# A RWKV time-mixing kernel: two head groups carried side by side through the chunk inverse, and a group norm that no longer takes its mean

## The chip, the cores and the metric

One core of one Trainium2 chip runs the whole program. Times are device microseconds (us) of one execution. Engines are named as in the profile: PE (TensorE matmuls), PEld (its weight loads), DVE (VectorE), ACT (ScalarE), POOL (GpSimd), SP (SyncE, which issues the weight transfers). PSUM is the memory PE writes; it has eight banks of 512 fp32 words a partition.

## What is computed

A block of 256 tokens with 1024 channels goes through a first block and then four layers; layers 0 and 3 mix over time with RWKV-7 (16 heads of 64 channels), and only this part is changed. In the reference, for each head and token:

```
def step(state, inp):
    r_t, w_t, k_t, v_t, kk_t, a_t = inp
    sa = jnp.einsum('bhvk,bhk->bhv', state, -kk_t)
    state = (state * w_t[:, :, None, :]
             + sa[..., None] * (kk_t * a_t)[:, :, None, :]
             + v_t[..., None] * k_t[:, :, None, :])
    return state, jnp.einsum('bhvk,bhk->bhv', state, r_t)
...
mean = jnp.mean(y, axis=-1, keepdims=True)
var = jnp.mean(jnp.square(y - mean), axis=-1, keepdims=True)
y = ((y - mean) * lax.rsqrt(var + RW_GN_EPS)).reshape(bsz, seq, d) * ln_w + ln_b
bonus = jnp.sum(rh * kh * r_k, axis=-1, keepdims=True) * vh
out = ((y + bonus.reshape(bsz, seq, d)) * g).astype(h.dtype) @ w_o
```

The mean and the variance are over a head's 64 values of one token. `y` is linear in `v`, channel by channel of the head.

## The kernel before

The program is a chain of stages. Each is a block of its own: every engine runs its list of instructions in order, waits on counted semaphores, and all meet at the block's end. A layer with time mixing runs a feed-forward half, `rwkv_wide_stage` (r, v, k), `rwkv_scale_stage` (decays and scalings, L2633 to L2828), `rwkv_chunk_stage` (L2831), `rwkv_norm_stage` (L3242), `output_stage` and the other feed-forward half.

**The chunk stage** cuts the 256 tokens into two chunks of 128 and the 16 heads into two groups of 8, so four pairs n = (chunk, group) are worked through one after the other. For a pair it needs the inverse of a unit-triangular 128x128 matrix per head. That is built from the two 64x64 diagonal blocks: PE makes the products of a and b (L2882, and transposed L2892), DVE masks them out of PSUM (L3138, L3139) and makes the first level of the inverse T and of its transpose (L3146 to L3154, `first_level`). Then come five levels, each doubling the size of the inverted blocks:

- POOL masks the matrix for the level (L3124), PE multiplies it with T (`level_x`, 16 products of 64x64, L3003), ACT copies the result to SBUF (L3074);
- PE multiplies back for T (L3013; not in the fifth level) and for its transpose (L3018), 16 products of 64x64 each, and DVE adds these (L3182, L3184, `level_sums`). The next `level_x` waits for both sums.

A level is thus one chain PE, ACT, PE, DVE. The rest of a pair's work (turning k, b and v to token-major, L2904; the products with k, L2917, and their masked copies, L3161; the products for c, L2941, for u, L2954, with b and r, L2923, for the carry, L2961, for y, L2977 and L2978, and for the state) is put between the level steps of the *next* pair, by hand, in the loop over n at the end of the PE, ACT and DVE lists. So the first pair's inverse has nothing beside it, and the last pair's other products come alone after the last level. PSUM: the levels use banks 0 to 2, the rest banks 3 to 7.

**The norm stage** sums each head's y per token on PE (L746 in `sums_by_token`, 16 products of 128x128 by 128x2), scales (DVE L3289), spreads the mean back (PE L755 in `spread_by_token`), subtracts it (DVE L3292), squares (ACT L3282), sums the squares (PE L746 again), takes the inverse root (DVE L3294, ACT L3284, DVE L3296), spreads it (L755), multiplies, adds the bonus and gates (DVE L3308, L3301, L3303).

**Weights** come through a ring of four slots of 3 MB, `load_ahead` (L439) on SP's queue; a unit waits until the one four before it is freed. The scale stage issues up to the unit three past its own last one (L2652). Units 62 and 63 (layer 0) hold the output weights; 64, the third past, is the next feed-forward half's first. The scratch of the chunk stage is one idle ring slot and three of the ten 1 MB buffers.

Of the kernel before, what the change touches and what calls it, by code (L numbers as in the profile page):

```python
# [22 lines left out]
P = 128  # L23
SEQ = 256
# [2588 lines left out]
def rwkv_scale_stage(core, n, h, dx, x_w, x_g, x_a, r, k, v, lw, a, g):  # L2613
# [19 lines left out]
    with core.nc.Block() as block:  # L2633
# [197 lines left out]
def rwkv_chunk_stage(core, r, k, v, a, b, level_bufs, solve_buf, wide):  # L2831
# [5 lines left out]
    ab_, t_, tt, ab21 = ([piece(level_bufs, 4 * n + q) for n in range(2)] for q in range(4))  # L2837
    x_, masked, c_in, u_ = (piece(solve_buf, q) for q in range(4))
    ak_t, rk_t, rb_t = (wide[:, q * 1024:(q + 1) * 1024].rearrange("p (h t) -> p h t", h=8) for q in range(3))
    tok = wide[:, 3072:4608].rearrange("p (q c m) -> p q c m", q=3, c=4)  # L2840
    state = core.state[:, 0, :].rearrange("p (c m) -> p c m", m=HEAD)
    scaled = core.state[:, 1, :].rearrange("p (c m) -> p c m", m=HEAD)
    bank = lambda q: core.psum[:, q, :]
    zeros = core.zeros
# [4 lines left out]
    groups = [(ck, g) for ck in range(SEQ // P) for g in range(2)]  # L2849
    N, L = len(groups), LEVELS - 1  # L2850
# [5 lines left out]
    pairs_of = lambda banks: banks.rearrange("p b (c t) -> p c b t", c=4)  # L2856
    turned_half = lambda h, half: other[half.start] if h % 2 else half
    with core.nc.Block() as block:
        names = ("turned", "turned_sb", "ab_products", "ab_sb", "ba_products", "t_ready", "k_products", "k_sb",
                 "rb_products", "rb_sb", "level_mask", "level_x", "level_x_sb", "level_t", "level_t_sb", "level_tt",  # L2860
                 "level_tt_sb", "c_sums", "c_sb", "u1_sums", "u1_sb", "carry_sums", "carry_sb", "u2_sums", "u2_sb",
# [4 lines left out]

        @block.tensor
        def _(pe):
            def rows(x, n, h):
                ck, g = groups[n]  # L2870
                return x[HEAD * (h % 2):HEAD * (h % 2) + HEAD, 4 * g + h // 2, ck * P:(ck + 1) * P]

            def a_and_r(n, h):
                ck, g = groups[n]
                at = (4 * g + h // 2) * SEQ + ck * P
                return core.bufs[HEAD * (h % 2):HEAD * (h % 2) + HEAD, 0:5:4, at:at + P]

            def products_ab(n):
                if n >= 2:
                    wait(pe, "rb_sb", n - 1)  # L2880
# [15 lines left out]
            def turn_operands(n):  # L2896
                ck, g = groups[n]
                now = slice(ck * P, (ck + 1) * P)
                if n:
                    wait(pe, "y_sb", n)  # L2900
# [912 lines left out]
```

## Time and profile before

| what | value |
|---|---|
| three runs | 3466.52, 3467.67, 3473.76 us; median 3467.67 |
| profiled execution, first to last instruction (span) | 3464.7 us; its own device time is not listed, so the median's 3.0 us more is taken as what lies around a span |
| busy, share of the span | PE 91%, PEld 85%, DVE 67%, ACT 46%, POOL 4% |
| chunk stage, layers 0 and 3 | 154.2 and 144.7 us |
| norm stage, layers 0 and 3 | 25.2 and 25.3 us |

A PE row's x counts two passes for an fp32 product (L3003's 16 products are x32) and one for a transpose. Its busy time is start to modelled end; groups overlap a little at their ends, so a group's cost in PE's queue is read from its start to the next group's start. PEclk is the granted clock of PE: 1.00 is 2.4 GHz, 0.50 is 1.2 GHz.

### The profile page before, as it was taken

The page shows a single profiled execution, that of the slowest core. Times are in us where ns is not written, and L with a number is a line of the kernel's source. Part 1 is how long each engine was busy: PE and PEld are TensorE (multiplying, and loading weights), DVE is VectorE, ACT ScalarE, POOL GpSimd, SP SyncE. Part 2 cuts the span into 40 slices and gives each one's busy share as a digit, 9 for nine tenths or more (in the row PEclk, how much of TensorE's full clock was granted, in tenths as well). Part 3 has the DMA queues.
Part 4 walks back from the last instruction along what each step waited for, and adds up shares of the span by engine and source line. Part 5 has one row for each costly group of instructions (what it writes and reads, how often), then busy time and mean ns, then how long its engine had stood idle before and what let it go on. Part 6 is the DMA issues. An engine that isn't in the chain of part 4 may idle for free. (4 is left out here: it accounts for less than half of the span.)

```text
span 3464.7 us, 62893 instructions
## 1 busy us (share of the span) xinstructions
PE 3157.3 (91%) x26416; PEld 2942.4 (85%) x26416; DVE 2335.4 (67%) x3486; ACT 1580.8 (46%) x2255; POOL 130.5 (4%) x148
## 2 busy tenths in 40 slices
PE   7679999889987799999989899999899999978899
PEld 5568777789876789999987899999699998867899
DVE  6547999767774467677577577775667677564544
ACT  3326777644551244544552444444644444432443
POOL 0000000000102000000000000000000001011000
PEclk9778999989997989999996899999899999989899
DMA  9336999757520047677430277675157575310242
GB/s 391 138 134 263 368 370 365 291 211 303 204 104 2 2 191 305 244 289 295 173 146 1 116 281 277 249 303 194 40 226 303 224 304 227 112 38 2 110 183 85
DMA packets 74502, 698.32 MB, mean 202 GB/s; under 512 B 8096, under 2 KB 12192, under 8 KB 50848
## 3 DMA queue, kind: packets, MB, share of 16 engines
q1 hardware_dynamic: 31360, 533.52, 39.3%
q10 hardware_dynamic: 41760, 153.11, 11.6%
q0 software_dynamic: 1152, 8.39, 0.6%
q8 instruction: 173, 2.83, 0.3%
q14 instruction: 57, 0.47, 0.0%
HBM read 690.79 MB, written 4.19 MB: 201 GB/s over the span
## 5 line engine op out<-in xcount | busy, mean ns | idle before, releaser
L1186 DVE TENSOR_TENSOR w_split<-ring,w_split 128x1024 fp32r<-128x1024 f32 x513 | 626.3, 1223 | 407.6 <-ACT w_split L1097 405.1
L1097 ACT ACTIVATE w_split<-ring 128x1024 fp32r<-128x1024 f32 x513 | 540.6, 1056 | 774.7 <-PE banks L1027 580.6
L1025 PE MATMUL banks<-u_split,w_split 128*128 128x256 f32 x2816 | 805.7, 286 | 14.7 <-DVE u_split L1246 12.9
L1026 PE MATMUL banks<-u_split,w_split 128*128 128x256 f32 x2816 | 803.8, 285 | 0.0
L1027 PE MATMUL banks<-u_split,w_split 128*128 128x256 f32 x2816 | 803.5, 285 | 0.0
L1025 PEld LDWEIGHTS banks<-u_split,w_split 128*128 128x128 f32 x2816 | 548.2, 195 | 19.4 <-DVE w_split L1186 10.0
L1026 PEld LDWEIGHTS banks<-u_split,w_split 128*128 128x128 f32 x2816 | 548.1, 195 | 0.4
L1027 PEld LDWEIGHTS banks<-u_split,w_split 128*128 128x128 f32 x2816 | 547.7, 195 | 0.0
L584 DVE CUSTOM_DVE_ANT_0 bufs<-bufs 128x1024 f32<-128x1024 f32 x332 | 395.0, 1226 | 41.9 <-DMA bufs<-ada 25.0
L1025 PE MATMUL banks<-h_split,w_split 128*128 128x256 f32 x1408 | 398.7, 283 | 1.8 <-DVE w_split L1186 1.8
L1026 PE MATMUL banks<-h_split,w_split 128*128 128x256 f32 x1408 | 398.4, 283 | 0.0
L1027 PE MATMUL banks<-h_split,w_split 128*128 128x256 f32 x1408 | 398.4, 283 | 0.0
L520 PE MATMUL banks<-bufs_split,ring_split 128*128 128x256 f32 x1312 | 381.0, 290 | 0.0
L518 PE MATMUL banks<-bufs_split 128*128 128x256 f32 x984 | 293.4, 298 | 55.2 <-DVE ring_split L506 37.1
L2129 DVE TENSOR_TENSOR ring_split<-ring,bufs_split 128x1024 fp32r<-128x1024 f32 x240 | 293.9, 1266 | 22.8 <-ACT bufs_split L2010 22.3
L519 PE MATMUL banks<-bufs_split 128*128 128x256 f32 x936 | 275.2, 294 | 0.0
L1025 PEld LDWEIGHTS banks<-h_split,w_split 128*128 128x128 f32 x1408 | 270.3, 192 | 2.5 <-issue 2.5
L1026 PEld LDWEIGHTS banks<-h_split,w_split 128*128 128x128 f32 x1408 | 270.3, 192 | 0.0
L1027 PEld LDWEIGHTS banks<-h_split,w_split 128*128 128x128 f32 x1408 | 270.3, 192 | 0.0
L2010 ACT ACTIVATE bufs_split<-ring 128x1024 fp32r<-128x1024 f32 x240 | 250.1, 1063 | 32.7 <-PE banks L1876 29.3
L520 PEld LDWEIGHTS banks<-bufs_split,ring_split 128*128 128x128 f32 x1312 | 262.5, 200 | 0.0
L518 PEld LDWEIGHTS banks<-bufs_split 128*128 128x128 f32 x984 | 199.9, 203 | 65.4 <-DVE ring_split L506 40.1
(472 smaller groups left out, 5067.5 us busy)
## 6 DMA issues: line engine op xcount, KB each, us to landing
ring<-stream SPq DMA_DIRECT2D x155, 3072.0 KB, 10.9
bufs<-ada ACTq DMA_DIRECT2D x288, 512.0 KB, 10.6
bufs<-ada SPq DMA_DIRECT2D x7, 2048.0 KB, 11.9
bufs<-ada POOLq DMA_DIRECT2D x8, 1024.0 KB, 8.3
ring<-stream SPq DMA_DIRECT2D x2, 2688.0 KB, 9.7
bufs<-c_rows SPq DMA_DIRECT2D x9, 512.0 KB, 4.5
ring<-stream SPq DMA_DIRECT2D x1, 2704.0 KB, 12.9
ring<-stream SPq DMA_DIRECT2D x1, 2176.0 KB, 7.8
```

Source lines behind the costliest of these rows:

```text
L518: pe.matmul(out, w_high, x_high, start=start, stop=False, skip_group_check=True)
L519: pe.matmul(out, w_high, x_low, start=False, stop=False, skip_group_check=True)
L520: return pe.matmul(out, w_low, x_high, start=False, stop=stop, skip_group_check=True)
L584: dve.tensor_tensor_reduce(w, w, c_row, 1.0, 0.0, ALU.mult, ALU.add, into).then_inc(done.sem, 1)
L1025: pe.matmul(out, w(0), x(0), start=start, stop=False, skip_group_check=True)
L1026: pe.matmul(out, w(0), x(1), start=False, stop=False, skip_group_check=True)
L1027: return pe.matmul(out, w(1), x(0), start=False, stop=stop, skip_group_check=True)
L1097: nc.scalar.activation(w_split[:, slot, 0, :], piece(j, b), ACT.Copy).then_inc(high.sem, 1)
L1186: e = nc.vector.tensor_tensor(w_split[:, slot, 1, :], piece(j, b), w_split[:, slot, 0, :].bitcast(F32), ALU.subtract)
L2010: act.activation(w_high[number % 4], piece(j, b), ACT.Copy).then_inc(high.sem, high.count(1))
L2129: dve.tensor_tensor(low_piece(j, b), piece(j, b), w_high[number % 4].bitcast(F32), ALU.subtract)\
```

## The change

- The two groups of a chunk go through the inverse side by side: each level does `level_x` for group 0 and 1, other products of both groups, the products back for group 0 and 1, other products again. Group g has PSUM banks 2g and 2g+1 for the levels and 4+2g and 5+2g for the rest; every scratch tile exists once a group.
- The first chunk's inverse now has its own turning and its products with k, with b and r, and the next chunk's ab and ba beside it; the second chunk's has the first's c, u, carry, y and state products, then its own turning and products with k. The second chunk's c, u, rb, carry and y products for both groups come after the last level.
- The ab and ba products are made as 64x64 blocks, only those that are used (24 and 16 a group in place of 8 and 8 of 128x128); DVE takes them with one full-width instruction in place of two half-width ones.
- v is turned by a matmul with `centering`, the identity less each head's mean, in place of a transpose, so y comes out with mean zero. One DVE instruction makes `centering`. ACT writes y's square beside y (one more activation a pair).
- The norm stage loses the mean: its sum, scale, spread, subtraction and squares. Its ACT list adds the first bias, takes the root, then adds the other biases.
- The scratch takes a second ring slot, so unit last + 3 is issued in the norm stage and no longer in the scale stage.

```diff
-            core.load_ahead(sync, (f"g2{n}", 1))
+            core.load_ahead(sync, None, core.place[(f"g2{n}", 1)][0] + SLOTS - 1)
...
-                    last = pe.matmul(bank(6 + h % 2)[:, (h // 2) * P:(h // 2 + 1) * P], rows(b, n, h), rows(a, n, h),
+                    for half in blocks:
+                        pe.matmul(banks(g)[half, h % 2, pair_at(h)], rows(b, n, g, h, half), rows(a, n, g, h, half), start=True, stop=True)
+                    last = pe.matmul(banks(g)[lower, h % 2, second_at(h)], rows(b, n, g, h, lower), rows(a, n, g, h, upper),
                                      start=True, stop=True)
...
+            def turn_v(n, g):
+                wait(pe, "padded", 1)
+                wait(pe, "kb_turned_sb", through(n, g))
+                for c in range(4):
+                    last = pe.matmul(banks(g)[:, 0, c * P:(c + 1) * P], v[:, 4 * g + c, n * P:(n + 1) * P], centering,
...
+            def level_x(n, g, level):
+                wait(pe, "level_mask", level_through(n, g, level))
                 if level == 1:
-                    wait(pe, "t_ready", n + 1)
-                else:
-                    wait(pe, "level_t_sb", n * (L - 1) + level - 1)
-                if m:
-                    wait(pe, "level_tt_sb", m)
+                    wait(pe, "t_ready", through(n, g))
+                if n or level > 1:
+                    wait(pe, "level_t_sb", level_through(n, g, level) - 2)
                 for h in range(8):
                     for half in blocks:
-                        last = pe.matmul(bank(1 + h % 2)[turned_half(h, half), pair_at(h)], masked[half, h, :], t_[n % 2][half, h, :],
+                        last = pe.matmul(level_banks(g)[turned_half(h, half), h % 2, pair_at(h)], masked[g][half, h, :], t_[g][half, h, :],
                                          start=True, stop=True)
                 done(last, "level_x")
 
-            def level_t(n, level):
-                m = n * L + level - 1
-                wait(pe, "level_x_sb", m + 1)
+            def level_t(n, g, level):
+                wait(pe, "level_x_sb", level_through(n, g, level))
                 if level < L:
                     for h in range(8):
                         for half in blocks:
-                            last = pe.matmul(bank(h % 2)[turned_half(h, half), pair_at(h)], tt[n % 2][half, h, :], x_[half, h, :],
+                            last = pe.matmul(level_banks(g)[turned_half(h, half), h % 2, pair_at(h)], tt[n][g][half, h, :], x_[g][half, h, :],
                                              start=True, stop=True)
-                    done(last, "level_t")
-                for h in range(8):
-                    for half in blocks:
...
+            behind_x = ({1: turn_k_and_b, 2: lambda n, g: products_with_k(n, g, 0), 3: products_rb,
+                         4: lambda n, g: products_ab(n + 1, g), 5: lambda n, g: products_ba(n + 1, g)},
+                        {1: lambda n, g: c_products(n - 1, g), 2: lambda n, g: carry_products(n - 1, g), 3: lambda n, g: y_products(n - 1, g),
+                         4: turn_k_and_b, 5: lambda n, g: products_with_k(n, g, 0)})
+            behind_t = ({1: turn_v, 2: lambda n, g: products_with_k(n, g, 1)},
+                        {1: lambda n, g: u_products(n - 1, g, 0), 2: lambda n, g: u_products(n - 1, g, 1),
+                         3: lambda n, g: state_products(n - 1, g), 4: turn_v, 5: lambda n, g: products_with_k(n, g, 1)})
+            for n in range(2):
+                for level in range(1, LEVELS):
+                    for g in both:
+                        level_x(n, g, level)
+                    for g in both:
+                        behind_x[n][level](n, g)
+                    for g in both:
+                        level_t(n, g, level)
+                    if level in behind_t[n]:
+                        for g in both:
+                            behind_t[n][level](n, g)
+            for g in both:
+                c_products(1, g)
+            for g in both:
+                u_products(1, g, 0)
+            for g in both:
+                products_rb(1, g)
+            for g in both:
+                carry_products(1, g)
+            for g in both:
+                u_products(1, g, 1)
+            for g in both:
+                y_products(1, g)
...
+                    act.activation(here(squares), y, ACT.Square)
+                    done(act.activation(here(r), y, ACT.Copy), "y_sb")
...
+            for g in both:
+                ab_copies(0, g)
+                first_level(0, g)
+            done(dve.scalar_tensor_tensor(centering, core.const("heads"), -1.0 / HEAD, ident, ALU.mult, ALU.add), "padded")
+            level_sums(0, 1)
+            k_copies(0, 0)
+            level_sums(0, 2)
+            k_copies(0, 1)
+            rb_copies(0)
+            level_sums(0, 3)
+            for g in both:
+                ab_copies(1, g)
+            level_sums(0, 4)
+            level_sums(0, 5)
+            for g in both:
+                first_level(1, g)
+            level_sums(1, 1)
+            carries(0)
+            level_sums(1, 2)
+            level_sums(1, 3)
+            states()
+            level_sums(1, 4)
+            k_copies(1, 0)
+            level_sums(1, 5)
+            k_copies(1, 1)
+            rb_copies(1)
+            carries(1)
     core.end_stage()
...
-                last = sums_by_token(core, pe, y, c, 0, RW_HEADS)
-            last.then_inc(mean.sem, mean.count(1))
-            pe.wait_ge(mean_ready.sem, mean_ready.at(1))
-            for c in range(KC):
-                last = spread_by_token(core, pe, mean_bank(c // 2)[:, c % 2, :], values, c, RW_HEADS)
-                if c % 2:
-                    last.then_inc(mean_spread.sem, mean_spread.count(1))
-            for c in range(KC):
-                pe.wait_ge(squared.sem, squared.at(c // 2 + 1))
-                last = sums_by_token(core, pe, tmp, c, 5, RW_HEADS)
+                last = sums_by_token(core, pe, squares, c, 5, RW_HEADS)
             last.then_inc(summed.sem, summed.count(1))
...
-            for q in range(KC // 2):
-                act.wait_ge(centered.sem, centered.at(q + 1))
-                act.activation(pair(tmp, q), pair(cent, q), ACT.Square).then_inc(squared.sem, squared.count(1))
...
+            with_bias(0)
             act.wait_ge(scaled.sem, scaled.at(1))
             act.activation(values, values, ACT.Sqrt).then_inc(rooted.sem, rooted.count(1))
+            for q in range(1, KC // 2):
+                with_bias(q)
...
-            dve.wait_ge(mean.sem, mean.at(1))
-            dve.tensor_scalar(values, core.psum[:, 0, 0:2 * RW_HEADS], -1.0 / HEAD, None, ALU.mult).then_inc(mean_ready.sem, mean_ready.count(1))
-            for q in range(KC // 2):
-                dve.wait_ge(mean_spread.sem, mean_spread.at(q + 1))
-                dve.tensor_tensor(pair(cent, q), pair(y, q), mean_bank(q), ALU.add).then_inc(centered.sem, centered.count(1))
...
-                dve.scalar_tensor_tensor(cent[:, c, :], cent[:, c, :], core.col(f"ln_w{n}")[:, c:c + 1], root_bank(c), ALU.mult, ALU.mult)\
+                dve.scalar_tensor_tensor(cent[:, c, :], y[:, c, :], core.col(f"ln_w{n}")[:, c:c + 1], root_bank(c), ALU.mult, ALU.mult)\
```

How the instructions stand on PE, in order. The names: `bufs` and `ring` are SBUF scratch, `banks` is PSUM. First place, the first two levels of the first inverse, from the ba products on. Before:

```order
L2892 MATMUL banks<-bufs 128x128 x8
L3003 MATMUL banks<-bufs 64x64 x16
L3013 MATMUL banks<-bufs 64x64 x16
L3018 MATMUL banks<-bufs 64x64 x16
L3003 MATMUL banks<-bufs 64x64 x16
L3013 MATMUL banks<-bufs 64x64 x16
L3018 MATMUL banks<-bufs 64x64 x16
```

Now:

```order
L3016 MATMUL banks<-ring 64x64 x32
L2915 MATMUL banks<-consts_sb,bufs 128x128 x16
L3025 MATMUL banks<-ring 64x64 x16
L3033 MATMUL banks<-ring 64x64 x16
L3025 MATMUL banks<-ring 64x64 x16
L3033 MATMUL banks<-ring 64x64 x16
L2922 MATMUL banks<-small,bufs 128x128 x8
L3016 MATMUL banks<-ring 64x64 x32
L2933 MATMUL banks<-bufs 128x256 x8
L3025 MATMUL banks<-ring 64x64 x16
L3033 MATMUL banks<-ring 64x64 x16
L3025 MATMUL banks<-ring 64x64 x16
```

L3016, L3025 and L3033 are the old L3003, L3013 and L3018, for two groups; L2915 turns k and b, L2922 turns v, L2933 is the old L2917. They stood behind the second pair's levels.

Second place, what PE does after the last level, up to the products for y. Before, one group (the other was done beside the last inverse):

```order
L2904 MATMUL banks<-consts_sb,bufs 128x128 x12
L2917 MATMUL banks<-bufs 128x256 x8
L2936 MATMUL banks<-zeros_split 128x256 x2
L2938 MATMUL banks<-state,bufs 128x64 x8
L2941 MATMUL banks<-ring 128x64 x8
L2954 MATMUL banks<-bufs 64x64 x8
L2923 MATMUL banks<-bufs 128x128 x8
L2961 MATMUL banks<-bufs 64x64 x8
L2954 MATMUL banks<-bufs 64x64 x8
L2972 MATMUL banks<-zeros_split 128x512
L2974 MATMUL banks<-bufs,state 64x128 x8
```

Now, both groups, behind the last L3033 and L2933:

```order
L2955 MATMUL banks<-zeros_split 128x256 x2
L2957 MATMUL banks<-state,bufs 128x64 x8
L2960 MATMUL banks<-ring 128x64 x8
L2955 MATMUL banks<-zeros_split 128x256 x2
L2957 MATMUL banks<-state,bufs 128x64 x8
L2960 MATMUL banks<-ring 128x64 x8
L2973 MATMUL banks<-ring 64x64 x16
L2942 MATMUL banks<-bufs 128x128 x16
L2981 MATMUL banks<-bufs,spare 64x64 x16
L2973 MATMUL banks<-ring 64x64 x16
L2991 MATMUL banks<-zeros_split 128x512
L2993 MATMUL banks<-bufs,state 64x128 x8
```

L2955, L2957, L2960 make c, L2973 u, L2942 the products with b and r, L2981 the carry, L2991 and L2993 begin y. Turning and the products with k no longer stand here, but everything from c on stands here for two groups.

Third place, SP's queue in layer 0, as one piece of the difference; L2633 ends the scale stage, L3269 and L3262 begin and end SP's list of the norm stage:

```order
 L2650 UNCONDITIONAL_BRANCH
 L452 DMA ring<-stream 128x2048
+L2633 UNCONDITIONAL_BRANCH
+L3269 UNCONDITIONAL_BRANCH
 L452 DMA ring<-stream 128x6144
-L2633 UNCONDITIONAL_BRANCH
+L3262 UNCONDITIONAL_BRANCH
 L1723 UNCONDITIONAL_BRANCH
 L452 DMA ring<-stream 128x6144 x2
```

The 3 MB transfer moves past the scale and the chunk stage into the norm stage.

## Rows read from the trace of the kernel before

**Rows 1.** Stretches: chunk and norm stages; last two, chunk stages up to the clock's rise.

```profile
core 0: us, PE busy (x) PEld busy (x) DVE busy (x) ACT busy (x) POOL busy (x), PEclk, DMA share, GB/s
1035.20:1189.40 154.20, 119.88 (x2614) 106.55 (x2614) 69.97 (x120) 29.91 (x56) 25.39 (x20) 0.82 0.03 10
1189.40:1214.60 25.20, 18.13 (x192) 17.57 (x192) 11.97 (x23) 7.33 (x14) 0.00 (x0) 0.79 0.01 2
3058.70:3203.40 144.70, 109.98 (x2614) 97.02 (x2615) 69.94 (x120) 29.93 (x57) 25.39 (x20) 0.90 0.01 2
3203.40:3228.70 25.30, 18.13 (x192) 17.55 (x192) 11.98 (x23) 7.31 (x14) 0.00 (x0) 0.85 0.00 1
1035.20:1066.50 31.30, 20.91 (x428) 19.33 (x430) 11.50 (x18) 2.39 (x4) 6.33 (x5) 0.50 0.10 41
3058.70:3078.30 19.60, 11.70 (x224) 10.71 (x224) 8.75 (x14) 1.19 (x2) 3.80 (x3) 0.51 0.01 2
```

**Rows 2.** Timeline, layer 3, a level at the low clock (start us, us, engine, ...).

```profile
3067.18 1.13 PE L3003 MATMUL banks<-bufs 64*64 64x64 f32 x32 [4.69 <-DVE bufs L3154]
...
3069.02 1.13 PE L3013 MATMUL banks<-bufs 64*64 64x64 f32 x32 [0.71 <-ACT bufs L3074]
...
3069.93 1.92 PE L3018 MATMUL banks<-bufs 64*64 64x64 f32 x32
...
3072.73 1.13 PE L3003 MATMUL banks<-bufs 64*64 64x64 f32 x32 [0.88 <-DVE bufs L3184]
```

**Rows 3.** Timeline, layer 3, a level with other products beside it, full clock.

```profile
3112.36 0.69 PE L3003 MATMUL banks<-bufs 64*64 64x64 f32 x32
...
3113.18 0.60 ACT L3074 ACTIVATE bufs<-banks 128x512 f32<-128x512 f32 x1 [2.76 <-PE banks L3003]
...
3113.83 0.69 PE L3013 MATMUL banks<-bufs 64*64 64x64 f32 x32 [0.32 <-ACT bufs L3074]
...
3114.35 1.10 PE L3018 MATMUL banks<-bufs 64*64 64x64 f32 x32
...
3115.49 0.69 DVE L3184 TENSOR_TENSOR bufs<-bufs,banks 128x512 f32<-128x512 f32 x1 [0.21 <-PE banks L3018]
```

**Rows 4.** Timeline, layer 3, from the ba products' copies to the next inverse's start.

```profile
3090.15 1.39 DVE L3146 TENSOR_TENSOR bufs<-banks,consts_sb 64x512 f32<-64x512 f32 x2 [0.40 <-PE banks L2892]
...
3094.27 0.69 PE L3003 MATMUL banks<-bufs 64*64 64x64 f32 x32 [4.17 <-issue]
...
3094.90 2.80 PE L2904 MATMUL banks<-consts_sb,bufs 128*128 128x128 f32 x12
```

**Rows 5.** Timeline, layer 3, the last pair's products, one after the other.

```profile
3178.07 0.51 PE L2972 MATMUL banks<-zeros_split 128*128 128x512 f32 x1
...
3181.58 0.60 ACT L3074 ACTIVATE bufs<-banks 128x512 f32<-128x512 f32 x1 [4.03 <-PE banks L2978]
...
3182.23 1.53 PE L2904 MATMUL banks<-consts_sb,bufs 128*128 128x128 f32 x12 [0.69 <-ACT bufs L3074]
...
3183.69 2.38 PE L2917 MATMUL banks<-bufs 64*128 64x256 f32 x16
...
3184.87 2.53 DVE L3161 TENSOR_TENSOR ring<-banks,consts_sb 128x512 f32<-128x512 f32 x4 [5.34 <-PE banks L2917]
...
3187.46 0.50 PE L2936 MATMUL banks<-zeros_split 128*128 128x256 f32 x2 [1.39 <-DVE ring L3161]
...
3188.93 2.00 PE L2941 MATMUL banks<-ring 128*128 128x64 f32 x16
...
3192.18 0.68 PE L2954 MATMUL banks<-bufs 64*64 64x64 f32 x16 [1.25 <-ACT bufs L3085]
...
3192.79 1.16 PE L2923 MATMUL banks<-bufs 64*128 64x128 f32 x16
```

**Rows 6.** Timeline, layer 0, norm stage: first and second sum, the root.

```profile
1189.43 3.70 PE L746 MATMUL banks<-consts_sb,bufs 128*128 128x2 f32 x32 [0.94 <-PEq L2858]
...
1198.73 3.73 PE L746 MATMUL banks<-consts_sb,bufs 128*128 128x2 f32 x32
...
1200.22 1.28 ACT L3284 ACT_TABLE_LOAD   x1
1202.50 0.19 DVE L3294 TENSOR_SCALAR small<-banks 128x32 f32<-128x32 f32 x1 [2.96 <-PE banks L746]
```

**Rows 7.** Page, DMA issues: size and us from issue to landing.

```profile
ring<-stream SPq DMA_DIRECT2D x155, 3072.0 KB, 10.9
```

More of the change, by code:

```diff
@@ L2828, in rwkv_scale_stage, with rwkv_chunk_stage @@
     core.end_stage()
-def rwkv_chunk_stage(core, r, k, v, a, b, level_bufs, solve_buf, wide):
+def rwkv_chunk_stage(core, r, k, v, a, b, squares, wides, tails, rest, centering):
     s = core.small
@@ L2896, in turn_operands, with products_ba @@
[L2896 to L2900, printed above, removed]
-                wait(pe, "t_ready", min(n + 2, N))
-                for q, (x, to) in enumerate(((k, 3), (b, 4), (v, 5))):
-                    for c in range(4):
-                        last = pe.transpose(bank(to)[:, c * P:(c + 1) * P], x[:, 4 * g + c, now], ident)
+            def products_ba(n, g):
+                out = banks(g) if n else level_banks(g)
+                if n:
+                    wait(pe, "ab_sb", through(n, g))
+                for h in range(8):
+                    for half in blocks:
+                        last = pe.matmul(out[half, h % 2, pair_at(h)], rows(a, n, g, h, half), rows(b, n, g, h, half), start=True, stop=True)
+                done(last, "ba_products")
@@ new lines, in turn_k_and_b @@
+            def turn_k_and_b(n, g):
+                if n:
+                    wait(pe, "y_sb", through(n - 1, g))
+                    wait(pe, "state_sb", through(n - 1, g))
+                else:
+                    wait(pe, "ab_sb", through(n, g))
+                for q, x in enumerate((k, b)):
+                    for c in range(4):
+                        last = pe.transpose(banks(g)[:, q, c * P:(c + 1) * P], x[:, 4 * g + c, n * P:(n + 1) * P], ident)
+                done(last, "kb_turned")
@@ L2915, in products_with_k, with products_rb @@
                 for h in range(4 * part, 4 * part + 4):
                     at = (h // 2 - 2 * part) * SEQ
-                    last = pe.matmul(bank(first + h % 2)[:, at:at + SEQ], rows(k, n, h), a_and_r(n, h), start=True, stop=True)
+                    last = pe.matmul(banks(g)[:, h % 2, at:at + SEQ], rows(k, n, g, h), a_and_r(n, g, h), start=True, stop=True)
                 done(last, "k_products")
-            def products_rb(n):
-                wait(pe, "c_sb", n + 1)
+            def products_rb(n, g):
+                if n:
+                    wait(pe, "u1_sb", through(n, g))
+                else:
+                    wait(pe, "k_sb", 4 * n + 2 + g + 1)
@@ L3141, in first_level @@
[L3141 to L3147 removed]
+            spread = lambda m: m.unsqueeze(1).unsqueeze(1).to_broadcast([m.shape[0], 4, 2, HALF])
@@ L3186, in scale_state @@
-            def scale_state(n):
-                ck, g = groups[n]
-                if ck:
+                for g in both:
+                    wait(dve, "k_products", 4 * n + 2 * part + g + 1)
+                    heads = slice(4 * part, 4 * part + 4)
+                    sums = banks(g).rearrange("p b (c a t) -> p c b a t", c=2, a=2)
+                    for out, which in ((ak_t[g], 0), (rk_t[g], 1)):
+                        last = dve.tensor_tensor(by_pair(out[:, heads, :]), sums[:, :, :, which, :],
+                                                 causal[:, which, :].unsqueeze(1).unsqueeze(1).to_broadcast([P, 2, 2, P]), ALU.mult)
+                    done(last, "k_sb")
```

461 lines of the change are left out of this document (200 added, 261 removed).

## The prediction, made before the change was run

> **What bounds the kernel now.** I read the stretches first, stage by stage. The two chunk stages take 154.2 and 144.7 us and the two norm stages 25.2 and 25.3 [rows 1]; the rest of the program is not touched. In a chunk stage DVE is busy 70 of 145 us, ACT 30, POOL 25 and PE 110, so no engine is full; DMA is near zero, so weights don't bound it. PE's clock is the second thing to see: 0.50 in the first 31.3 us of layer 0's stage and the first 19.6 us of layer 3's [rows 1], where the first inverse runs alone; 0.82 and 0.90 over the stages. The timeline then shows what a level costs. Alone and at the low clock, from one L3003 to the next, it is 5.55 us, of which PE's queue works 0.91 (L3013) and some 1.9 (L3018) and about 1.1 (L3003), the rest being ACT's copy, DVE's sum and the handovers [rows 2]. At the full clock, with others' products between, the same steps are 0.52 (L3003, L3013) and 1.03 (L3018), and the chain from L3003 to L3013 is 1.47, 0.60 of it ACT [rows 3]. So the stage is a chain of latencies, four pairs one after another, with a bare inverse at the front and a bare pair of product groups at the back (3182.23 to 3203.4, 21 us). The norm stage is a plain chain too.
>
> **The norm stage.** Between the first sum's start and the second's lie 9.30 us [rows 6], and nothing else than the mean is in them: sum, scale, spread, subtraction, squares. They go; the second sum and all behind it stay. ACT could be late with the root: its table load now comes after two biases (0.8), so it ends at 2.1 us after the start, and the scale is due 3.77 after its sum's start (L746 to L3294) [rows 6]. Covered. The other six biases run beside PE's spread. Term: 2 x -9.3 = -18.6. If the load ended late, its 1.28 would show, once a stage.
>
> **Costs of product groups at full clock,** start to next start, for one group of heads: turning 12 tiles 1.46, so 0.12 each; k products 2.3 for both parts; c in the first chunk 1.9, in the second 3.4 (from L2936 on: 1.47 + 1.9); u 0.6; rb 1.1; y in the second chunk 3.25 (from L2972 to ACT's copy, less the handover), in the first, where the state is zero, some 1.8; k's masked copies on DVE 2.55 [rows 5]. Carry: as u, 0.6. Four inverse products back (two groups) T = 2 x (0.52 + 1.03) = 3.1; two `level_x` X = 1.0 [rows 3].
> New forms, bounded: a 64x64 product costs 0.032 where the sixteen spread over all four quarters of the array (L3013) and 0.065 where they use two (L3018) [rows 3]. The 24 of ab use three quarters in turn: between 0.8 and 1.6 a group, I take 1.2, near the old 1.1. The 16 of ba use all four: 0.5 to 1.0, I take 0.55. State, 16 products on two quarters, 1.0. v by matmul: between a transpose's 0.12 and twice L2941's 0.24 [rows 5], I take 0.24, so 1.0 a group, where transposes were 0.5. DVE's full-width copies: 0.69 as L3184's 128x512, not 1.39 as L3146's two [rows 3, 4]; so a first level is 4.0 - 0.7 = 3.3 and ab copies 1.4. `centering` 0.35 on DVE, covered; the square, 0.60 of ACT, is covered but for one at the end.
>
> **The new chunk stage, marked at each start of the products back.** Head, low clock: ab 2.4 (1.2 at half rate); DVE in line for both groups 1.4 + 3.3 + 1.4 + 3.3, with handovers 9.6; second `level_x` 0.9; 16 turnings at 2.80/12 = 0.23 [rows 4], 3.6. Together 16.5. Then
> - first chunk, level 1 to 2: T 3.1, v 1.9, X 1.0, k 2.3 = 8.3; to 3: 3.1 + k 2.3 + X 1.0 + rb 2.2 = 8.6;
> - to 4, with nothing behind T: the second group waits T 3.1, handovers 0.4, two sums 1.4, its own X 0.5, = 5.4; ab 2.4: 7.8; to 5: 5.4 + ba 1.1 = 6.5;
> - to the second chunk: PE waits for DVE, first products 1.3 with handover, sums 1.4 + 0.3, two first levels 6.6, X 0.6, c 3.8 = 14.0;
> - to 2: T 3.1, u 1.2, X 1.0, carry 1.2 = 6.5; to 3: 3.1 + u 1.2 + X 1.0 + y 3.6 = 8.9; to 4: 3.1 + state 2.0 + 1.0 + turning 2.0 = 8.1; to 5: 3.1 + v 1.9 + 1.0 + k 2.3 = 8.3;
> - behind: L3033 2.1, k 2.3, wait for copies 0.5, c 6.8, ACT's copies and u 2.1, rb, its copy and the carry 4.5, the carry's copy and u 1.8, y 6.5, square and copy 1.5 = 28.1.
> Sum 16.5 + 105.1 = 121.6. Two checks: the same bookkeeping with the old order and layer 3's clock gives 145 against 144.7 measured; and PE's queue alone, summed, is about 97, so 122 is not impossible.
> Beside it the clock. Both old stages fell low again after PE stood idle: after the 4.17 us of one first level the next 2.80 us of turning ran at about half rate [rows 4]. The new stage has one such hole, twice as long, before the second chunk, and small ones at the end. A stretch of 7 us at half rate there costs 1.5 to 2.5. And the first rise came at 19.6 in one layer and 31.3 in the other; PE is dense in the new stage from 12 us on, so I take about 16 in one and 20 to 25 in the other, 2 to 3 more. Layer 3: 123; layer 0: 126. Bounds: 118 (full clock from the start) and 133 (low to 32 us, and twice again).
> Terms: 123 - 144.7 = -21.7, 126 - 154.2 = -28.2.
>
> **The rest.** Where the stall goes: the last level's end is now followed by 28 us in one line, where 26 were before, so the tail doesn't shrink; it is the third and fourth pair's chains that vanish. The weight unit issued in the norm stage lands 10.9 us after issue [rows 7], inside the 16 us left of it, and it is the next feed-forward half's; the output stage, which comes between, has its units. So 0. If that cover failed it would be up to 10.9 a layer. ACT, DVE and POOL work beside PE.
>
> **Sum.** -18.6 - 21.7 - 28.2 = -68.5 on the profiled span of 3464.7: 3396. The median of the runs is 3.0 above that span, so 3399 us.
>
> **Rivals.**
> - DVE becomes the bound. For: both groups' sums (2.8) and both groups' masked k copies (5.1, in two halves) are in one in-order list, so a copy of other work stands ahead of a sum that `level_x` waits for; by my marks the copies of level 2 end 0.1 us before the sum is due. Against: DVE totals 65 of 122 (70 less the copies and first levels that shrink, four times 1.4). The Trainium skill (TensorEngine Tiling (Array Packing), PSUM Bottleneck) says that packing speeds up TensorE but not the evacuation of PSUM, which may then bound; the 4.17 us hole agrees with it. Price: half a k copy (1.3) at each of ten levels, 13 a stage, 3425.
> - PE's quarters get in each other's way (ab 1.6, ba 1.0, v 0.45 each): over four pairs 1.6 + 1.8 + 3.4, about 7 a stage, 3413. Inside the range.
> - Side by side only in name: the groups' waits serialise them. Then only the norm's term is left: 3449. Against: own banks, tiles and counts for each group.
> - The slower side: PE idles in each wait often enough that its clock stays at 0.50 through the stage. All PE costs are then about 1.8 times (L3018 1.9 for 1.03), and by the same marks a stage takes 190: 380 - 299 - 18.6 = +62, 3530. It decides from 159 us a stage on, some 107 us of it low. For: 31 us low in layer 0. Against: PE has more work in less time, and the old stage of layer 3 had 0.90 with less. The Trainium skill (TensorE: Matmul & The Clock Gate, Part 1) reports a kernel whose short idles between product groups made the clock swing between its two levels; the drop in [rows 4] agrees in kind.
> - The clock rises at once and stays: 118 a stage, 3386.
>
> **Chances.** Forecast, within 3388 to 3416, 0.81; above, up to 3449, 0.11; below 3388, 0.06; slower 0.02. Range 3388 to 3416: it takes in both clock bounds but the ends, and the quarters' case. A change of under 0.2% (7 us) can't be told from none here; so faster 0.97, same 0.01, slower 0.02.
>
> **What would show it.** After: chunk stages of 120 to 128 us; L3016's x32 runs close together, with the pairs of ACT copies; PE idle some 7 us before the second chunk's second `level_x`, broken only by the first, and DVE busy there; PEclk near 0.95 after the first 20 us; the norm stage at 16 us; no wait on the ring's first unit behind the output stage. Wrong: DVE copies ahead of late sums (L3192 in place of the sums) at most levels, or PEclk at 0.50 past 40 us.

## Result, and the profile after

| | before | after |
|---|---|---|
| median (range, runs) | 3467.1 (3461.9 to 3473.8, 4) | 3411.9 (3408.0 to 3413.3, 4) |
| profiled span | 3464.7 | 3406.2 |
| ratio of times | | 0.985, 95% interval 0.9833 to 0.9866 |

The forecast was 3399, in 3388 to 3416. The kernel is 55 us faster where 68 were forecast. First the windows of the changed kernel (us of the stretch, then busy time and count of PE, PEld, DVE, ACT and POOL, PE's clock, DMA share, GB/s): chunk and norm stage of layer 0, of layer 3, and two stretches inside layer 3's chunk stage.

```profile
1034.56:1163.33 128.77, 106.12 (x2822) 98.17 (x2823) 66.62 (x113) 31.40 (x61) 25.26 (x20) 0.87 0.01 3
1163.33:1180.90 17.57, 10.45 (x97) 10.15 (x97) 9.20 (x19) 4.79 (x10) 0.00 (x0) 0.77 0.46 180
3020.69:3153.07 132.38, 109.14 (x2822) 100.98 (x2823) 66.72 (x113) 31.41 (x61) 25.33 (x20) 0.85 0.01 3
3153.07:3170.16 17.09, 10.20 (x96) 9.88 (x97) 9.03 (x18) 4.79 (x11) 0.00 (x0) 0.78 0.47 185
3077.50:3094.60 17.10, 13.94 (x218) 13.58 (x220) 5.42 (x8) 3.47 (x8) 2.53 (x2) 0.50 0.01 2
3094.60:3142.20 47.60, 43.59 (x1171) 40.19 (x1166) 25.11 (x49) 15.45 (x30) 7.52 (x6) 1.00 0.01 3
```

The chunk stages took 128.8 and 132.4 us (154.2 and 144.7 in [rows 1]), the norm stages 17.6 and 17.1 (25.2 and 25.3). That is 25.4 + 12.3 + 7.6 + 8.2 = 53.5 of the 58.5 us between the spans. The other 5.0 lie in code that is the same: in the twelve profiles of the changed kernel and its variants the first chunk stage starts between 1031.2 and 1041.4 us, so a time of the whole program moves by that much on its own, and the experiments below are read by their stages. A stage moves too: the unedited changed kernel's four chunk stages in two profiles (e8_after_again is the second) took 128.8, 132.4, 130.8 and 129.0 us. A gain of some 3 us in the mean of two stages is thus only just above that spread.

The fifth row is the surprise: 17.1 us in the middle of the stage at a clock of 0.50, with PE busy 13.9 of them. It will be called the low stretch, and the place ahead of it, between the two chunks, where PE waits twice, the hole. Here is the hole in layer 3's timeline (start, us, engine, line, ...): DVE's first levels for the second chunk (L3167 to L3175), `level_x` of either group (L3016) and the first chunk's c products (L2960).

```profile
3073.67 0.69 DVE L3207 TENSOR_TENSOR ring<-ring,banks 128x512 f32<-128x512 f32 x1 [0.24 <-PE banks L3033]
3074.27 0.68 DVE L3167 TENSOR_TENSOR ring<-banks,consts_sb 128x512 f32<-128x512 f32 x1
...
3075.30 0.85 DVE L3171 TENSOR_TENSOR ring<-ring,consts_sb 64x256 f32<-64x256 f32 x2
...
3076.80 0.69 DVE L3175 TENSOR_TENSOR ring<-ring,consts_sb 128x512 f32<-128x512 f32 x1
3077.40 0.69 DVE L3167 TENSOR_TENSOR ring<-banks,consts_sb 128x512 f32<-128x512 f32 x1
...
3077.59 1.13 PE L3016 MATMUL banks<-ring 64*64 64x64 f32 x32 [3.96 <-DVE ring L3175]
...
3078.43 1.93 DVE L3171 TENSOR_TENSOR ring<-ring,consts_sb 64x256 f32<-64x256 f32 x2
3078.82 1.26 POOL L3145 TENSOR_TENSOR ring<-ring,consts_sb 128x512 f32<-128x512 f32 x1 [6.53 <-PE banks L3016]
...
3081.01 0.68 DVE L3175 TENSOR_TENSOR ring<-ring,consts_sb 128x512 f32<-128x512 f32 x1
...
3081.80 1.13 PE L3016 MATMUL banks<-ring 64*64 64x64 f32 x32 [3.07 <-issue]
...
3082.86 7.09 PE L2960 MATMUL banks<-ring 128*128 128x64 f32 x32
```

PE waits 3.96 us for DVE, does one `level_x` and waits 3.07 more. Then the 16 c products (x32, two passes each) take 7.09 us; at the full clock the same take 3.8 (below). And L3171's two instructions are 0.85 for group 0 and 1.93 for group 1, where POOL's mask (L3145) runs beside them from 3078.82 on.

The stage against the forecast, step by step (from one start of the products back to the next, us; the first from the stage's first product):

| step | forecast | layer 0 | layer 3 |
|---|---|---|---|
| head | 16.5 | 17.9 | 17.9 |
| level 1 to 2 / 2 to 3 | 8.3 / 8.6 | 8.3 / 7.9 | 8.5 / 7.9 |
| 3 to 4 / 4 to 5 | 7.8 / 6.5 | 6.7 / 7.1 | 9.2 / 7.3 |
| to the second chunk (the hole) | 14.0 | 20.0 | 18.3 |
| 1 to 2 | 6.5 | 8.2 | 7.9 |
| 2 to 3 / 3 to 4 / 4 to 5 | 8.9 / 8.1 / 8.3 | 9.2 / 8.0 / 7.9 | 10.8 / 8.0 / 7.9 |
| behind the last level (the tail) | 28.1 | 27.4 | 28.6 |
| sum | 121.6 | 128.8 | 132.4 |

Where others' products stand beside the levels the forecast holds within 1.1 us, but for two steps of layer 3: 9.2 for 7.8 and 10.8 for 8.9. In these PE stands still in the middle of its products for 2.04 us, and for 1.10 and 0.57 us, with nothing it waits for (last section). The excess is 1.4 at the head and 6 to 8 in the hole and the step behind it; in layer 0 a standstill of 1.51 us just ahead of the hole is in it.

### The profile page after: what moved, and what is told of

The parts are those of the page before. It is cut to its first block and busy times, and to the rows that moved or that the text cites. A ratio compares the mean times of both kernels' runs of the same rounds, so it can differ in the third digit from the quotient of the medians.

```text
span 3406.2 us, 63313 instructions
## 1 busy us (share of the span) xinstructions
PE 3120.0 (92%) x26640; PEld 2917.2 (86%) x26640; DVE 2322.7 (68%) x3462; ACT 1578.9 (46%) x2255; POOL 130.3 (4%) x148
## 6 DMA issues: line engine op xcount, KB each, us to landing
ring<-stream SPq DMA_DIRECT2D x1, 2704.0 KB, 13.7
```

## The experiments

Each is an edit of the changed kernel. Three theories of the excess: A, PE's clock behind the hole; B, DVE's copies in their one list; C, the time that the products themselves take in PE's queue. D is a part of the hole: POOL's mask beside DVE.

### Filling the hole, and its sizes

```diff
+            def fill(count):
+                wait(pe, "level_t_sb", level_through(0, 1, L))
+                for q in range(count):
+                    pe.matmul(level_banks(1)[:, q % 2, second_half], ident, v[:, q % 4, :], start=True, stop=True)
...
+                        if n and level == 1:
+                            fill((5, 6)[g])
                         level_x(n, g, level)
```

> Adds 11 products of 128x128 by 128x256 that nobody reads on PE before the second chunk: 5 before its first level_x of group 0 (after the last sum), 6 before that of group 1, into level banks that nobody reads then. Nothing waits longer for them unless they outlast DVE (11 x 0.43 at the full clock, 4.7 us of 7.0 idle). Theory A (the 12.4 us between my schedule and layer 3's measured stage is mostly a clock that stays at 0.50 for 17 us after PE's hole): the low stretch of 17 us behind the hole shrinks or goes, the row of the c products (7.09 us) falls to about 4, and a stage is 4 to 8 us shorter, the program 3396 to 3404. Theory B (DVE's copies and handovers are the excess): the clock may rise, the time stays within 2 us of 3412. Theory C (the excess is in PE's queue): 2 x 1 us slower, 3413 to 3416.

Measured: median 3408.4 (3393.6 to 3414.7), ratio 0.982 (0.9788 to 0.9852). The windows are its two chunk stages, the norm stage of layer 0, the hole's stretch and 13.6 us of layer 3's tail:

```profile
1039.63:1169.88 130.25, 112.81 (x2845) 102.72 (x2845) 66.72 (x113) 31.54 (x61) 25.35 (x20) 0.88 0.01 3
3031.98:3160.00 128.02, 112.59 (x2844) 102.98 (x2845) 66.63 (x113) 31.53 (x61) 25.34 (x20) 0.87 0.01 3
1169.88:1185.65 15.77, 8.76 (x96) 8.43 (x96) 9.02 (x18) 4.79 (x10) 0.00 (x0) 0.84 0.51 201
3081.90:3095.00 13.10, 10.85 (x154) 9.41 (x154) 7.90 (x13) 2.79 (x7) 2.54 (x2) 1.00 0.01 3
3133.20:3146.80 13.60, 13.40 (x112) 12.41 (x113) 1.54 (x2) 3.46 (x8) 0.00 (x0) 0.50 0.00 0
```

and rows of layer 3's timeline: added products, the c products of the first chunk, and of the tail's second group:

```profile
3086.50 2.86 PE L3023 MATMUL banks<-bufs,consts_sb 128*128 128x256 f32 x12
...
3090.71 3.79 PE L2960 MATMUL banks<-ring 128*128 128x64 f32 x32
...
3136.68 3.67 PE L2960 MATMUL banks<-ring 128*128 128x64 f32 x16
```

The clock stayed at 1.00 through the hole. The hole's step and the one behind it took 16.3 + 5.8 us in layer 0 and 14.6 + 5.8 in layer 3, against 28.2 and 26.2: **6 us less a stage**, and with the full clock layer 3's two steps are 20.4, as forecast (20.5). So A is right on what the low stretch costs. It is wrong on the stage, and on the time of 3396 to 3404: the clock fell in the tail instead, where only 0.53 us of idle stood ahead, the second group's L2960 took 3.67 (2.0 at full clock), and the tail 34.1 us for 27.4. What was won in the middle was given back. C finds nothing here: 4.7 us of added products lengthened neither step.

> e1_fill_hole with 60 and 80 products of 64x64 by 64x64 (0.032 us each, 4.5 us) in place of 5 and 6 of 128x128 by 128x256. There the clock stayed full at the hole and fell 45 us later, in the c products of the tail, for 13.7 us, with nothing but 0.5 us of idle ahead. If the size of the added products had brought that on: here no fall at 101 to 104 us of the stage, tail of 23 us, stages of 122 to 124 us. If it is the long stretch at the full clock: the same fall, stages of 128 to 130. If small products don't count as work for the clock: the 14 to 17 us low behind the hole stay.

Edit: the same `fill`, with products of 64x64 in turn over the four quarters, `fill((60, 80)[g])`. Median 3403.3 (3395.9 to 3410.1). Layer 3 did as before: full through the hole (14.9 + 5.8), then 13.6 us at 0.50 from 100.4 us of the stage on, tail 34.2, stage 127.3. The fall in the tail is thus not due to large products. Small ones did as well as large ones in layer 3, where 3.4 us of idle remained in three pieces; in layer 0, where 3.7 remained in four, the clock fell for 10.2 us behind the hole: stage 131.5.

> The changed kernel unedited, for its times beside the others on one chip and for a second profile. Theory A: 17 us at 0.50 behind the hole in both layers again, the full clock in the tail's c products, stages of 128 to 132 us. Rival: the clock's pattern is chance, and the low stretch is absent or elsewhere in one of the two layers.

Median 3417.1 (3409.9 to 3420.2, 6 runs); stages 130.8 and 129.0; 17.1 and 13.6 us low behind the hole, the tail's c products at the full clock. So A's pattern is no chance of one profile; the length of the low stretch varies, 13.6 or 17.1.

### The first level made earlier

```diff
+            for g in both:
+                first_tt(1, g)
+            for g in both:
+                first_t(1, g)
             level_sums(0, 5)
-            for g in both:
-                first_level(1, g)
```

(`first_tt` is the part of `first_level` that needs ab alone, `first_t` the part on the ba products.)

> The second chunk's first level is made on DVE before the last sums of the first chunk and no longer behind them: its transposed part after the sums of level 4, the rest as the ba products come. PE's hole (3.96 + 3.07 us of layer 3's stage) falls to about 1.5 us. Theory A: the hole's 5.5 us and the 6 to 8 us of low clock behind it both go, 10 to 13 us a stage, 3386 to 3392. Theory B (DVE is the bound): the same instructions only stand elsewhere in the list, the wait turns up before level 5's sums: 0 to 3 us a stage, 3406 to 3412. Without a clock effect: 5.5 us a stage, 3401.

Measured: median 3410.9 (3403.6 to 3416.9), stages 125.8 and 128.2. The hole fell from 7.0 to 3.9 and 4.8 us, and 13.7 us of low clock stayed behind it in both layers. Layer 3's timeline says why no more:

```profile
3075.21 0.96 DVE L3175 TENSOR_TENSOR ring<-ring,consts_sb 128x256 f32<-128x256 f32 x1
...
3076.18 1.83 DVE L3178 TENSOR_TENSOR ring<-ring,consts_sb 64x256 f32<-64x256 f32 x2
...
3078.05 0.69 DVE L3181 TENSOR_TENSOR ring<-ring,consts_sb 128x512 f32<-128x512 f32 x1
...
3080.59 0.68 DVE L3170 TENSOR_TENSOR ring<-banks,consts_sb 128x512 f32<-128x512 f32 x1
...
3083.24 1.28 DVE L3213 TENSOR_TENSOR ring<-ring,banks 128x512 f32<-128x512 f32 x2
...
3084.07 1.99 PE L3016 MATMUL banks<-ring 64*64 64x64 f32 x64 [4.84 <-DVE ring L3213]
```

DVE works without a break from 3075.2 to 3084.5, and a pair of its instructions again takes double beside POOL (L3178, 1.83). Here, for 9 us, B is true: moving work in DVE's list moves the wait. The gain is some 3 us a stage (127.0 in the mean for 130.2 of the changed kernel's two profiles), which the hole's 2.2 to 3.6 us account for, without the 6 that A promised with a shorter hole.

### POOL's mask held back

```diff
+                        if level == 2 and g == 0:
+                            wait(pool, "t_ready", through(n, 1))
                         done(pool.tensor_tensor(masked[g], ...), "level_mask")
```

> POOL's level-2 mask of group 0 waits until both first levels are made, in both chunks, so that DVE's instructions between SBUF tiles have no POOL instruction beside them. Theory D (POOL's mask doubles the time of DVE's instructions that touch SBUF alone): L3171 of group 1 falls from 1.9 to 0.85 and L3168 from 0.93 to 0.42 for its two instructions, the hole is 1.5 us shorter, a stage 1 to 3 us, 3406 to 3410. Rival: the slow ones are slow for their tile's shape or place: no change in them, and nothing or +1 us.

Median 3402.6 (3399.3 to 3411.5), stages 128.2 and 126.4. Layer 3's timeline at the same place as above:

```profile
3071.29 1.14 PE L3016 MATMUL banks<-ring 64*64 64x64 f32 x32 [3.95 <-DVE ring L3177]
...
3072.13 0.85 DVE L3173 TENSOR_TENSOR ring<-ring,consts_sb 64x256 f32<-64x256 f32 x2
...
3074.41 1.13 PE L3016 MATMUL banks<-ring 64*64 64x64 f32 x32 [1.99 <-issue]
3074.46 2.50 POOL L3147 TENSOR_TENSOR ring<-ring,consts_sb 128x512 f32<-128x512 f32 x2 [8.77 <-DVE ring L3177]
```

D is right: the pair (now L3173) takes 0.85 with POOL's mask behind it, and the second wait is 1.99 us for 3.07, in layer 0 2.43 for 3.49. That is 1.1 us of the hole. The Trainium skill (SBUF — State Buffer, Who interferes with whom) states that a DVE instruction with two inputs in SBUF contends with a GpSimd one that reads SBUF, over a pair of ports that is locked exclusively; 0.85 against 1.93 beside a mask of 1.26 agrees. The forecast took each duration from rows where POOL was idle.

### The old norm, and the head

> The chunk stage side by side as it is, but v turned by transposes, no square beside y, and the norm stage with its mean, as before the change. The norm stage is 25.2 again (25.2 and 25.3 before), against 17.6 and 17.1. The chunk stage loses 4 x 0.5 us of PE and 1.2 us of ACT at its end (0.6 to 2 us a stage). Theory of separate terms: 2 x 7.9 - 2 x 1.5 = +13, 3425. Rival (the forecast's 9.3 a stage is there but hidden in the chunk stage's end): +18.6 or more, 3431.

Edit: `turn_v` is a transpose again, `y_copies` writes no square, and the norm stage is the old one. Median 3423.9 (3420.6 to 3425.3); norm stages, by the windows,

```profile
1168.51:1193.65 25.14, 17.87 (x192) 17.29 (x192) 11.96 (x23) 7.31 (x14) 0.00 (x0) 0.84 0.32 126
3161.45:3186.63 25.18, 18.08 (x192) 17.49 (x192) 11.97 (x23) 7.31 (x14) 0.00 (x0) 0.85 0.32 126
```

chunk stages 127.4 and 127.9. The norm stage is back at its old length and the time is near the 3425 of the separate terms, so the norm's term is separate from the chunk's. In the changed kernel its stage is 17.6 and 17.1. In e1_fill_hole's layer 0, where the sum (L746) ran wholly at the full clock in 3.70 us, it is 15.8 at a mean clock of 0.84 (window above) against 0.77: there the forecast's 15.9 holds.

> In the first chunk each group's k and b are turned ahead of its first level_x, in the waits for DVE (1.9 and 5.3 us), and no longer behind both. Theory A (PE's queue and latencies as I book them): the 3.6 us of turning at the low clock go into idle time, the second level's level_x comes 3 us earlier (at 20.2 in place of 23.2 us of the stage), a stage is 3 us shorter. Rival (ACT: its copies of the turned tiles then meet the copies of level_x, or the clock falls for as long elsewhere): under 1 us a stage.

```diff
                     for g in both:
+                        if n + level == 1:
+                            behind_x[n][level](n, g)
                         level_x(n, g, level)
```

Median 3406.7 (3402.2 to 3407.2), stages 127.5 and 126.4. The second `level_x` came at 21.0 and 21.3 us in place of 23.2 and 23.4: 2.1 won of 3 expected. The rest went to the clock. The products back now start at 14.2 us of the stage in place of 17.9, and the clock rises at 18.5 and 19.2 as before (18.7 and 19.2), so they run at 0.50, and their step takes 9.9 and 10.2 us against 8.3 and 8.5. Group 1's second half of them in layer 3, here and in the changed kernel:

```profile
3037.19 1.83 PE L3033 MATMUL banks<-ring 64*64 64x64 f32 x32
3041.08 1.10 PE L3033 MATMUL banks<-ring 64*64 64x64 f32 x32
```

The turning has left the low clock, and other products have taken its place there. No row there has PE waiting for ACT's copies of the turned tiles.

### Together

> Three edits together: the second chunk's first level made ahead of the last sums (e2_early), in the first level of both chunks each group's other products ahead of its level_x, and POOL's masks kept off DVE's SBUF instructions (the level-2 mask behind both first levels, the second chunk's level-1 mask behind the transposed parts). Latencies: head -1.5 and -3 us, hole from 7.0 to about 1.5 us. If the low clock behind the hole is set by its length it goes too, -6: 14 to 16 us a stage, 3380 to 3385. If low clock of the same length turns up elsewhere in the stage, as in e1_fill_hole: 8 to 9 us a stage, 3393 to 3397.

The edits are those of the three sections above, the head's for both chunks, and POOL's first mask of the second chunk waits for the last `first_tt`. Median **3392.6** (3386.7 to 3401.1, 6 runs), against 3417.1 of the changed kernel on the same chip; ratio to before 0.9802 (0.9778 to 0.9826). Stages 117.2 and 122.0, so 20.6 of the 24.5 us between the medians show in the stages. In layer 0 the hole was 0.29 us and no low stretch followed; in layer 3 it was 1.97, and 10.2 us at 0.50 followed. POOL's masks were not kept off DVE altogether: beside them L3178 took 1.35 and 1.04 us, where the same instruction takes 0.69 alone.

> e6_combo with DVE's list before the second chunk in another order: group 0's whole first level, group 1's transposed part, group 0's last sum, the rest of group 1, its last sum. Group 0's c products can start 2 us earlier and its level_x 1.3 us earlier. Latencies: hole 0.4 to 2.0 us down to under 1, 0.5 to 1 us a stage. If the 10 us at 0.50 behind the hole in layer 3 of e6_combo came from its 1.97 us of idle, they go: 4 us more in that layer, 3386 to 3389. If a 2 us hole is not their cause: 3391 to 3393.

```diff
-            for g in both:
-                first_tt(1, g)
-            for g in both:
-                first_t(1, g)
-            level_sums(0, 5)
+            first_level(1, 0)
+            first_tt(1, 1)
+            level_sums(0, 5, (0,))
+            first_t(1, 1)
+            level_sums(0, 5, (1,))
```

> e6_combo unedited, for its times beside e9_order and a second profile. If the length of the idle ahead sets the low clock in the hole: layer 0 and layer 3 differ again only where their idle does. If chance sets it: low stretches of another length or in the other layer. Time 3390 to 3395.

e9_order: median **3384.4** (3379.1 to 3387.1, 5 runs), ratio 0.9771 (0.975 to 0.9792). e10_combo_again: 3397.4 (3387.2 to 3398.3), ratio 0.980 (0.9777 to 0.9824); its stages 115.6 and 121.1, again 0 and 10.2 us low, after 0.29 and 1.69 us of idle. So it is no chance that the layers differ; that the idle makes the difference fits, but is not shown by these two runs alone. The two kernels ran on the same chip, and only 3.2 us of the 13.0 between their medians are in the chunk stages (of the profiles): most of the rest is code that is the same, the first chunk stage starting at 1033.0 us in one profile and 1040.8 in the other. e9_order's windows, its stages and the two stretches in question:

```profile
1033.00:1147.80 114.80, 100.70 (x2822) 92.47 (x2823) 65.79 (x113) 31.19 (x61) 26.02 (x20) 0.95 0.01 3
3005.38:3124.20 118.82, 103.51 (x2823) 95.50 (x2823) 65.90 (x113) 31.14 (x61) 26.02 (x20) 0.92 0.01 3
3058.80:3065.60 6.80, 6.80 (x124) 6.56 (x118) 0.79 (x2) 1.90 (x5) 3.82 (x3) 0.50 0.01 4
3101.30:3124.20 22.90, 19.53 (x295) 17.02 (x295) 5.19 (x8) 6.83 (x15) 0.00 (x0) 1.00 0.01 1
```

The low stretch is 6.8 us behind 0.82 of idle, shorter but not gone, so of the two answers expected neither holds whole; layer 0's stage is at the full clock from 19 us on.

> e9_order with the eleven 128x128 by 128x256 products of e1_fill_hole put on PE ahead of the second chunk's first level_x of group 1, where there is hardly any idle to hide them (4.7 us at the full clock). If the fall at 101 to 104 us in e1_fill_hole came from the added products (more of PE's work in the stretch): the clock falls again for 10 to 14 us in the tail's c products and a stage is 4 to 5 + 5 to 6 us longer than e9_order's 114.8 and 118.8, 3402 to 3406. If it came from something else: the tail stays at the full clock, 4 to 5 us a stage, 3393 to 3395.

Edit: `fill(11)` ahead of the second chunk's `level_x` of group 1, in e9_order. Median 3388.0 (3386.9 to 3396.2), ratio 0.9766 (0.9747 to 0.9784).

```profile
1039.94:1162.94 123.00, 108.43 (x2845) 99.02 (x2845) 65.82 (x113) 31.23 (x61) 26.08 (x20) 0.92 0.01 3
3022.52:3141.32 118.80, 104.78 (x2844) 96.24 (x2845) 65.72 (x113) 31.11 (x61) 26.01 (x20) 0.95 0.01 3
3118.40:3141.30 22.90, 19.52 (x294) 17.00 (x295) 5.22 (x8) 6.82 (x14) 0.00 (x0) 1.00 0.01 2
```

In layer 3 the clock no longer fell, neither there nor in the tail: the hole's step and the next are 1.9 us longer than e9_order's (18.7 for 16.8), for 4.9 us of added products. (That the stage is 118.8 as there is luck: a gap of 1.8 us in the ab products, of the kind at the end of this text, is missing.) In layer 0, where nothing was to be won, 123.0 against 114.8: 5.1 in the hole's step, and 3.0 in a tail with 6.8 us low. So added products alone don't bring the fall in the tail, and neither does a long stretch at the full clock: e9_order's layer 0 had 99 us of it, longer than the 82 us before e1_fill_hole's fall. But the added products have a part, it seems: all four falls of 6.8 us or more in the tail stand in the six stages that have them (e1_fill_hole twice, e7_small_fill's layer 3, here layer 0), and none in the other 18, where the tail has at most 3.4 us low. **What else it takes stays open.**

## Why the forecast held, and where it was off

- **What bounds it: right.** The stage was a chain of latencies; four chains became two. DVE is busy 66.6 of 128.8 us, and no engine is full.
- **The marks: right** where products stand beside the levels, and in the tail. The new forms were priced right or a little high: a group's 24 ab products 1.2 forecast and 0.93 measured from start to start, ba 0.55 and 0.47, v 1.0 and 0.95.
- **The clock behind the hole: the term that failed.** "A stretch of 7 us at half rate there costs 1.5 to 2.5." The hole was found and its length (7 us) was right, but 17 us at 0.50 followed, and cost 6 (e1_fill_hole). The step that failed is the reasoning "one such hole, twice as long": it took the low stretch to grow with the hole. The old kernel, behind two holes of the same 4.17 us, one in each layer, was low for 6.8 and for 3.4 us:

```profile
1074.30:1081.10 6.80, 5.95 (x100) 5.53 (x102) 1.44 (x3) 2.17 (x4) 1.27 (x1) 0.50 0.00 0
3095.00:3098.40 3.40, 3.40 (x40) 3.07 (x44) 0.00 (x0) 1.26 (x3) 1.27 (x1) 0.50 0.02 5
```

  In the new order 3.86 us in e2_early's layer 0 brought 13.6. So the idle alone doesn't set the length, and what does stays open; that taking the idle away takes the stretch away is shown. The rest of layer 3's excess is no matter of this clock: 2.04 us of standstill make most of the 2.5 us by which its level 3 to 4 is longer than layer 0's, and 1.10 and 0.57 most of the 1.9 in level 2 to 3 of the second chunk. The forecast had no term for them.
- **The head: 1.4 us short,** of which DVE's doubling beside POOL made 1.0: with POOL held back the second wait is 4.32 us for 5.28, and the head 17.0 and 16.4 for 17.9 (16.4 where the clock also rose 3 us earlier).
- **"About 16" for the first rise: right in size** (18.7 and 19.2, with a rise of 3.4 us between, so low for some 15.5). The 2 to 3 more for layer 0 did not come: it was the quicker one.
- **The norm: -9.3 forecast, -7.6 and -8.2 measured.** Of the 1.7 and 1.1 us missing, the remaining sum at a partly low clock made 0.9 and 0.7 (L746 4.59 and 4.39 us for 3.70 in [rows 6]).
- **The weights' move: nothing, as forecast.** The stretch from the first norm stage's end to the second chunk stage is 1839.8 us for 1844.1 before, and PE's longest wait in its first 120 us is 6.2 us for 5.9.
- **Rivals.** DVE as the bound fell as a price on every level; it holds for the 9 us before the second chunk (e2_early). PE's quarters: no, by the measured prices above. "Its clock stays at 0.50 through the stage": the mechanism of the slower side was real, once a stage, for 17 us and not for 107, and its sign, 0.50 past 40 us, was there from 56 to 73 us. The Trainium skill's swing (TensorE: Matmul & The Clock Gate, Part 1), cited for that rival, is in every profile here: layer 0's stage is at 0.50 for 5.1 us, at 1.00 for 3.4, then at 0.50 for 10.3, at 1.00 for 37.5 and at 0.50 for 17.1.
- The sum, against the spans: the chunk stages gave 37.7 us for 49.9 (12.2 short), the norm 15.8 for 18.6 (2.8 short), and 5.0 came from code that did not change. That is 58.5 for 68.5; the median of the runs lies 5.7 above the profiled span where 3.0 were taken. Both chunk stages lie above the 120 to 128 us given as a sign, and the 5.0 are luck: without them the time would have been about 3417, just outside the range, and e8_after_again's median is 3417.1. The mechanism held, the range only just.

## To carry to other kernels

When two chains are put side by side, look for the one place where both wait at once: there PE idles longer than either did alone, and the low clock behind it can cost as much as the wait. Bring the waited-for work ahead of the last sums, in the order in which it is asked for, and give PE the group that is ready. Filler kept the clock up where it would have fallen, but no stage here was clearly shorter for it. And price an instruction in the company that it will have: a pair of DVE instructions between SBUF tiles took 1.93 us beside a POOL instruction and 0.85 alone.

## What the runs showed of the hardware

- Of the 24 chunk stages of twelve profiles, 12 had 3.8 us or more of idle in the hole, and in all of them 13.6 to 17.1 us at 0.50 followed; of eight with 0.7 to 3.7 us, four had 6.8 to 10.2 and four none; the four with under 0.4 had none. Time in added products is not counted as idle. PE was busy for 13.9 of layer 3's 17.1 us, and for 13.4 of the 13.6 us in e1_fill_hole's tail.
- A low stretch can move: filled away in one place it came back 45 us later, with 0.53 us of idle ahead.
- PE stands still for 0.6 to 2.0 us one to three times a stage inside a run of products, with nothing it waits for, 54 times in the 24 stages (counting those over 0.6 us). In e6_combo, layer 3, inside the ab products (L2893, L2894):

```profile
3048.24 0.22 PE L2894 MATMUL banks<-bufs 64*64 64x64 f32 x1
...
3050.46 0.21 PE L2894 MATMUL banks<-bufs 64*64 64x64 f32 x1 [2.01 <-issue]
```

  The trace has two transfers between 3045 and 3052 us, both of the instruction queue: one from 3047.6 to 3049.0, and one from 3051.5 on. PE goes on 1.4 us behind the first one's end. So it is each time: all 54 standstills end 1.2 to 1.6 us behind the end of such a transfer, while these transfers start 3.4 us or more apart (in the profiles of the changed kernel, e1_fill_hole, e6_combo and e9_order). That speaks strongly for instructions that arrive late; no run was made to change it.
- The mean clock of an execution and its time go together: e1_fill_hole's four runs had 0.930, 0.932, 0.933 and 0.938 at spans of 3412.8, 3407.8, 3405.4 and 3391.8 us.
